# The third attention component's first row-maximum pieces issued four products later, and two adaLN weight blocks issued ahead of the fourth operand stack

## The reference, cut to what matters

```
mod = silu(c) @ w_ada + b_ada                    # adaLN: shift, scale and gate, 6 * 1024 columns
h = rmsnorm(x) * (1 + sc1) + sh1
proj = h @ w_in                                  # retention q,k,v,gate; forgetting q,k,v; differential q,k,v
mix = concat(retention, forgetting attention, differential attention)
x = x + g1 * (mix @ w_out)
h = rmsnorm(x) * (1 + sc2) + sh2
x = x + g2 * (square(relu(h @ w_up)) @ w_down)

# differential attention: two softmaxes per head, each with its own 32-wide q and k
p = softmax(where(chunk mask, q @ k^T * scale, -inf))      # c = 0 and 1
out = (p[0] - lam * p[1]) @ v
```

## Time and profile before

| What | Value |
|---|---|
| median of three runs | 3326.7 us |
| span of the profiled execution (the only time that the profile gives for it) | 3325.1 us |
| PE busy | 3224.1 us, 97% of the span |
| DVE busy | 1696.0 us, 51% |
| ACT busy | 984.5 us, 30% |
| POOL busy | 957.8 us, 29% |
| mean granted clock of PE | 0.985 of full speed (1.00 is 2.4 GHz, 0.50 is 1.2 GHz) |
| bytes moved by DMA | 307.07 MB, 92 GB/s over the span |

### The profile page before, as it was taken

The page is one execution under the profiler, slowest core; times in us unless marked ns, Lnnn a source line. Parts: engine busy times, 40 slices in busy tenths (PEclk is TensorE's granted clock), DMA queues, the critical chain, the costliest instruction groups (busy, mean ns, idle before and its releaser), DMA issues.

```text
span 3325.1 us, 50329 instructions
## 1 busy us (share of the span) xinstructions
PE 3224.1 (97%) x19286; PEld 2894.2 (87%) x19286; DVE 1696.0 (51%) x3073; ACT 984.5 (30%) x1770; POOL 957.8 (29%) x690
## 2 busy tenths in 40 slices
PE   6999999899999999999999999999999999999998
PEld 3988897566799999999988879966678999999997
DVE  4746273674495555555573544156546633333335
ACT  3132222574451111111232313147635311111112
POOL 1312332221232333333332214212213233333332
PEclk8999999999999999999999999999999999999999
DMA  5512476535112222222222114563321011111112
GB/s 213 180 47 95 156 238 218 125 91 139 33 59 85 85 76 76 88 82 82 83 64 73 35 50 176 190 172 76 76 66 45 27 51 44 44 45 50 44 44 72
DMA packets 135351, 307.07 MB, mean 92 GB/s; under 512 B 53789, under 2 KB 74341, under 8 KB 131729
## 3 DMA queue, kind: packets, MB, share of 16 engines
q1 hardware_dynamic: 93584, 224.39, 23.4%
q10 hardware_dynamic: 41600, 80.44, 6.9%
HBM read 240.14 MB, written 57.90 MB: 90 GB/s over the span
## 4 chain that ended last, share of the span: by engine, by line
PE 90%; DVE 4%; SPq 2%; ACT 1%; ACTq 1%; issue 1%; DMA 1%; DVEq 0%
PE ps L1387 22%; PE ps L1358 19%; PE ps L1299 9%; PE ps L1232 8%; PE ps L1022 6%; PE ps L1212 5%; PE ps L1078 4%; PE ps L1169 3%; PE ps L1276 3%; PE ps L1004 2%; PE ps L1046 1%; DVE tn L2053 1%; PE ps L1334 1%; DVE h_lo L2066 1%; DVE x L2238 1%; PE ps L1113 1%
## 5 line engine op out<-in xcount | busy, mean ns | idle before, releaser
L768 POOL CAST w_hi<-raw 128x1024 fp32r<-128x1024 f32 x212 | 229.5, 1082 | 1862.5 <-PEq L1393 447.3
L2238 DVE SCALAR_TENSOR_TENSOR x<-ps,mod,x 128x352 f32<-128x352 f32 (+2 forms) x768 | 353.6, 489 | 431.5 <-PE ps L1387 351.5
L1387 PE MATMUL ps<-act_hi,w_hi 128*128 128x352 f32 x1536 | 496.0, 323 | 0.0
L1387 PE MATMUL ps<-act_hi,w_lo 128*128 128x352 f32 x1536 | 492.6, 321 | 0.0
L1387 PE MATMUL ps<-act_lo,w_hi 128*128 128x352 f32 x1536 | 492.1, 320 | 0.0
L1358 PE MATMUL ps<-h_hi,w_hi 128*128 128x352 f32 x1344 | 433.5, 323 | 0.0
L1875 ACT ACTIVATE relu_b<-ps,consts 128x352 f32<-128x352 f32 x192 | 106.4, 554 | 1103.5 <-PE ps L1358 1084.3
L1358 PE MATMUL ps<-h_hi,w_lo 128*128 128x352 f32 x1344 | 430.8, 320 | 0.0
L1358 PE MATMUL ps<-h_lo,w_hi 128*128 128x352 f32 x1344 | 430.4, 320 | 0.0
L1299 PE MATMUL ps<-pT,vb 128*128 128x512 f32 (+5 forms) x1080 | 401.3, 461 | 0.0
L2302 DVE TENSOR_REDUCE pm<-ps 128x1 f32<-128x512 f32 (+4 forms) x468 | 251.2, 548 | 243.3 <-PE ps L1169 158.8
(11 more groups left out here) (223 smaller groups left out, 6112.3 us busy)
## 6 DMA issues: line engine op xcount, KB each, us to landing
raw<-in_w SPq DMA_DIRECT2D x212, 512.0 KB, 3.6
ada_next<-in_w_ada SPq DMA_DIRECT2D x48, 512.0 KB, 4.2
ada_w<-in_w_ada SPq DMA_DIRECT2D x24, 512.0 KB, 5.9
kb<-scr_k SPq DMA_DIRECT2D x36, 328.0 KB
kb<-scr_k SPq DMA_DIRECT2D x120, 82.0 KB
qb<-scr_q SPq DMA_DIRECT2D x36, 264.0 KB
ada_nat<-in_w_ada_first SPq DMA_DIRECT2D x8, 1024.0 KB, 20.5
qb<-scr_q SPq DMA_DIRECT2D x120, 66.0 KB
```

Source lines behind the costliest of these rows:

```text
L768: pool.tensor_copy(hi, raw[:, uc % 2, 0:width]).then_inc(pool_hi, 1)
L1387: last = mm(ps[:, i % 6, 0:GW], w[:, k * 256 + o * 128:k * 256 + o * 128 + 128], (act_lo if low else act_hi)[:, k * T + g * GW:k * T + (g ...
L2238: last = v.scalar_tensor_tensor(xs, ps[:, bank, a - g * GW:b - g * GW], gs, xs, ALU.mult, ALU.add)
```

## The change

Two edits, and no instruction is added or removed. (The new lines shift the later line numbers of the file by up to 12: L1169, L1276 and L1299 are L1181, L1288 and L1311 afterwards.)

First, in `ring_table` the slot of a row piece now comes from `row_slot`. For component 2 alone it is the later one of the old slot `5 + r` and `9 + r // 2`. Pieces 0 to 3 move from slots 5, 6, 7, 8 to 9, 9, 10, 10; pieces 4 to 7 from 9, 10, 11, 12 to 11, 11, 12, 12; pieces 8 to 12 stay in 13 to 17. This holds in both layers.

Second, in layer 0 SP issues the adaLN blocks 24 and 25 right after stack 2, ahead of stack 3, and no longer at the first two components, behind stacks 3 to 7 and weight unit 38.

```diff
@@ -109,6 +109,13 @@
 PIECES = row_pieces()
 NR = len(PIECES)
 ROW_LEAD, TURN_LAG = 8, 2
+LATE_COMP, LATE_FROM = 2, 9
+
+
+def row_slot(u, r):
+
+    s = NP * (u - 1) + r - ROW_LEAD
+    return max(s, LATE_FROM + r // 2) if u == LATE_COMP else s
@@ -116,7 +123,7 @@
         for r in range(NR):
-            at.append((NP * (u - 1) + r - ROW_LEAD, 0, "row", u, r))
+            at.append((row_slot(u, r), 0, "row", u, r))
@@ -225,6 +232,7 @@
 ADA_PARTS_AT = [3, 8]
+ADA_SOON = 2
@@ -662,6 +670,10 @@
                     stack_load(li, u)
                     if u == 4:
                         value_load_(li, 1)
+                    if li == 0 and u == 2:
+                        for w in range(ADA_SOON):
+                            sp.wait_ge(ada_done, 2 * (19 + w) + 2)
+                            back_load(24 + w)
                 raw_load(li * NU + 38, 0)
@@ -669,7 +681,7 @@
-                    if li == 0 and u < 8:
+                    if li == 0 and ADA_SOON <= u < 8:
                         sp.wait_ge(ada_done, 2 * (19 + u) + 2)
                         back_load(24 + u)
```

## The result

The changed kernel takes 3310.6 us (median of 5 runs, 3308.11 to 3317.7) against 3326.7 us before: a ratio of 0.995, 95% interval 0.9938 to 0.9962. It gained 16.1 us where 27.1 were forecast, and its time lies above the stated range of 3295.5 to 3308.5 us. The profiled execution has a span of 3310.7 us, 14.4 us under that of before, at a mean clock of 0.988.

A forecast was written before the change was run, and what follows sets the result against it. PE, 97% busy, was taken as the bound, so only its stops and slow clock pay. Gains 6.8 + 8.6 + 12.3 less 0.6 for DVE made 27.1 us: span 3298.0, plus 1.6 to the median, 3299.6 us; range 3295.5 to 3308.5.

The forecast's parts named there:

- Stack 2 and slot 9: Component 2's moved pieces: stack 2 still lands at 566.00 in layer 0, leaving PE waits of 0.4 and 0.46 us.
- Block 24: Layer 0, slots 29 to 32: the earlier load ends DVE's wait and PE's 9.89 us; term 12.3 us with slow clock.
- Block 26: Layer 0 adaLN load behind stack 8: issued at about 608.4, there at 616.2, needed at 616.7 earliest; cost nothing.
- Slot 9 to slot 18 in layer 1: Attention window after the moved pieces: 18.85 us becomes 9.33 plus 0.9 for helper rows, gaining 8.6 us.
- with a busy queue they take about 0.9 us longer than PE leaves them: Component 1's helper rows, both layers: a charge of 0.9 us each, from 0 to twice that.
- the sign of being wrong that the prediction named: Slots 9 to 18: a PE clock under 0.95 would show the prediction wrong.
- catch up: Stacks after stack 3: PE needs 14.2 us per component, SP 6.6 us per stack, so later stacks are not late.
- Stack 3 late: Rival, chance 0.16: PE waits 1.7 to 4.7 us in slot 18 of layer 0; time 3301.3 to 3306.7 us.
- The second rival: Chance 0.08: clock falls after slot 9's short wait, or helper rows stop PE 2 us or more; 3306.6 us.
- The rule of the Trainium skill that I weighed: Each engine consumes one queue's descriptors in ring order, so stack 3 cannot pass the adaLN blocks; bound 4.8 us.
- the terms for the two waits: Attention gains: 6.8 and 8.6 us for stack 2's wait in layers 0 and 1, 12.3 us for block 24's.
- The lower end of the range: Takes DVE's 0.6, helper rows' 1.8 and slot 9's 0.9 us at nothing, less 0.8 for scatter: 3295.5 us.

The follow-up runs named there:

- e7: The paced kernel e5 with the two adaLN loads ahead of stack 3 again, as in the changed kernel; 3316.2 us, ratio 0.9965.
- e5: e3 with SP pacing the later stacks, mostly one per component, and unit 38 after component 3; stacks 11 and 12 together; 3311.3 us, ratio 0.9949.
- e3: The changed kernel with the two adaLN loads issued behind stack 3 and not ahead of it; 3306.8 us, ratio 0.994.
- e8: e5 with stack 12 issued after component 8, no longer straight behind stack 11 after component 7; 3296.5 us, ratio 0.9908.
- e4: The changed kernel with ACT sending each component's helper rows behind the exponential of product 7, not 9; 3315.5 us, ratio 0.9961.
- e6: e5 with each paced stack started some 5 products earlier, in flight together with the helper rows; 3301.9 us, ratio 0.9924.
- e10: The changed kernel run once more, nothing altered; 3311.8 us, ratio 0.9956.

## Why the prediction was wrong, step by step

- **Stack 2 and slot 9: right.** It landed at 566.09 (566.0 said); the waits left were 0.26 and 0.80 us (0.4 and 0.46).
- **Block 24: right.** DVE's wait and PE's 9.9 us went. Slot 18 to slot 32 gained 10.4 us (9.9 said). Block 26 was issued at 610.74 (608.4 said), and nothing waited for it.
- **Slot 9 to slot 18 in layer 1: right.** 9.60 us at a clock of 1.00, 10.2 said; the 0.9 us charged there for helper rows did not come.
- **The step that failed: "with a busy queue they take about 0.9 us longer than PE leaves them", in component 1 alone, and 1.8 us as its upper end.** In layer 0 PE waited 3.7 us for component 1's helper rows, and the clock fell behind it: 15.70 us from slot 9 to 18 in place of 10.2, at a mean clock of 0.78, which is the sign of being wrong that the prediction named (under 0.95). I bounded the latency by the longest in my rows, 3.34 us, though the edit put 1.05 MB ahead of those very DMAs; e7 against e5, on one chip, shows that this placement costs 4.9 us (3316.2 against 3311.3); e3 agrees within its scatter (3306.8 against 3310.6 and 3311.8).
- **The same step's scope.** I checked each later stack for landing in time, found them to "catch up", and charged nothing behind slot 18. They did land in time. What was late was the small DMA that shares the engines with them. Before, PE's stops of 5.3 us, and in layer 0 of 9.9 us, let SP run ahead. In layer 0 component 3 sent its helper rows from 613.2 on, long after the burst ended at 599.3; now it sends them at 600.2, inside it. In layer 1 component 4 sent them at 2232.5, between the end of the burst (2230.5) and the start of stack 8 (2236.2); now stack 8 follows the burst without a pause, and it is still being worked off when they are sent. Those stretches lost 3.8 us in layer 0 and 6.1 in layer 1. Rows sent into the burst are not always late: component 3 in layer 1 sent them into it before the change as well, and did not wait. e8 gives 14 to 15 us back by moving issue times alone, with the bytes and the programs of PE, DVE and ACT unchanged.
- **Rivals.** "Stack 3 late" did not happen, although 1 MB stood ahead of it. It was not put to the full test, because PE reached slot 18 at 581.79 and not at 576.2; but the last packet of stack 3 had ended at 574.3, 3.9 us later than before the change. The second rival was the nearest: helper rows that stop PE for 2 us or more, and the clock falling there. I gave it 0.08 and priced only the slow clock behind such a wait, 7.0 us in the first window of each layer (3306.6 us), not the wait itself and no place behind slot 18. The rule of the Trainium skill that I weighed (page "DMA: Bandwidth & Descriptors", section "Queues, rings and completion order", ring order within a queue) was held against SP's stacks only. The same section says that an engine takes turns between its queue rows, a whole packet of several descriptors at a time; by that a 4.5 KB DMA on ACT's queue would wait for the packet in hand and not for all that SP has queued. The traces here show 5.7 to 8.8 us for it, so being on another queue did not protect it from a wait; how many descriptors the engines took in one turn they do not show.
- **Sum.** 3299.6 us was forecast; e8, which has both edits, another order of SP's loads and no waits for helper rows, takes 3296.5. So the terms for the two waits were of the right size, and the one for helper rows was too small. The lower end of the range also takes off 0.9 us of waiting in slot 9, which the sum never charged; that has no part in the miss.

Why the engines take up the 18 packets of ACT's queue only after packets of SP's stays open: the packet records give times and queues, and not which of the 16 engines served a packet or how it chose. A single engine with a longer backlog than the mean share shows is therefore not excluded.

## What to carry to other kernels

When a stall is removed, list every small transfer that the later work waits for, and ask what the issuing queues will have in flight when it is sent at its new, earlier time: the stall may have been what kept that transfer clear of the burst. A latency read from a calm stretch is no bound for a stretch into which the edit moves a megabyte. Prefetches that have slack are worth pacing, one per unit of compute, even if each of them is already early enough.

## What the runs showed of the hardware

- A 4.5 KB DMA from ACT's queue took 2.4 us or less from the end of its issue to its use at a DMA share of 0.69, 3.3 at 0.72 with a stack in flight, 5.7 in a stretch whose share fell from 0.98 to 0.64, and 7.0 at shares of 0.99 to 1.07; in e4, sent right behind stack 8, it took 8.8 us.
- In the changed kernel the last of its packets starts 0.7 us after the end of the issue in 25 of 36 components, and 2.5 to 4.9 us after it in the four that made PE wait more than 1 us.
- One 972 KB stack beside it cost at most 0.5 us (e6); two stacks and value tiles in a row, issued just ahead of it, cost 4.1 us (e5), and nothing when they were issued some 5 products earlier (e6).
- A PE wait of 3.7 us was followed by 8 us at a mean clock of 0.67; waits under 1 us left the clock at 1.00 (e6, e8). Between them it went either way: 1.00 after 1.56 us (2217.72 to 2222 in the changed kernel), 0.61 after 1.47 us (2219.58 to 2224 in e10).
- Issuing two small DMAs between ACT's exponentials two products earlier cost PE about 0.6 us per component in layer 0 (e4).
